# One product of 512 columns for an operand's two parts in the last feed-forward stage, and a final normalisation over transposed tokens

## The reference, cut to what matters

```python
def swiglu(h, w_in, w_out):
    gate, up = jnp.split(h @ w_in, 2, axis=-1)
    return (jax.nn.silu(gate) * up) @ w_out

def layer_norm(x):
    mu = jnp.mean(x, axis=-1, keepdims=True)
    var = jnp.mean(jnp.square(x - mu), axis=-1, keepdims=True)
    return (x - mu) * lax.rsqrt(var + EPS)

# the last two lines of the second block, last layer
x = layer_norm(ALPHA * x + 0.5 * g3 * swiglu(x * (1.0 + sc3) + sh3, ffn2_w_in[1], ffn2_w_out[1]))
return x
```

## Time and profile before

| | us |
|---|---|
| median of 3 runs | 2087.27 (2086.97 to 2087.86) |
| profiled execution | 2088.37 |
| its span (first to last instruction) | 2086.6 |
| TensorE busy | 2052.6 |
| VectorE busy | 1373.0 |
| ScalarE busy | 752.9 |
| GpSimd busy | 150.7 |

### The profile page before, as it was taken

The page is one execution under the profiler, slowest core; times in us unless marked ns, Lnnn a source line. Parts: engine busy times, 40 slices in busy tenths (PEclk is TensorE's granted clock), DMA queues, the critical chain, the costliest instruction groups (busy, mean ns, idle before and its releaser), DMA issues. The chain is left out here.

```text
span 2086.6 us, 30241 instructions
## 1 busy us (share of the span) xinstructions
PE 2052.6 (98%) x12718; PEld 1784.8 (86%) x12718; DVE 1373.0 (66%) x2160; ACT 752.9 (36%) x934; POOL 150.7 (7%) x136
## 2 busy tenths in 40 slices
PE   9999999999999999999999999999999999999998
PEld 8979979888888988688888888988888899779998
DVE  5965975776775657557776775655555565666555
ACT  4464465221222544436221222521221242555333
POOL 0400500000002000020000002000000200010001
PEclk9999999999999999999999999999999999999999
DMA  6744654554543210322554543333442333124542
GB/s 239 242 146 141 243 171 159 187 198 162 200 170 123 98 40 6 107 81 108 189 198 162 201 170 123 122 139 109 176 151 90 123 153 141 41 65 154 189 171 90
DMA packets 69280, 301.39 MB, mean 144 GB/s; under 512 B 6176, under 2 KB 24224, under 8 KB 49184
## 3 DMA queue, kind: packets, MB, share of 16 engines
q1 hardware_dynamic: 66432, 290.06, 39.2%
q10 hardware_dynamic: 2720, 9.51, 1.2%
HBM read 298.50 MB, written 1.05 MB: 144 GB/s over the span
## 5 line engine op out<-in xcount | busy, mean ns | idle before, releaser
L446 PE MATMUL PS<-xh,wh 128*128 128x512 f32 (+1 forms) x3676 | 1008.8, 349 | 2.7 <-DVE OA L1827 0.9
L446 PEld LDWEIGHTS PS<-xh,wh 128*128 128x128 f32 x3676 | 663.4, 189 | 92.6 <-issue 1.5
L446 PE MATMUL PS<-xl,wh 128*128 128x512 f32 (+1 forms) x2086 | 710.6, 341 | 0.0
L358 ACT ACTIVATE wh<-raw 128x2048 fp32r<-128x2048 f32 (+4 forms) x221 | 377.3, 1708 | 314.2 <-PE PS L446 232.3
L362 DVE TENSOR_TENSOR wh<-raw,wh 128x2048 fp32r<-128x2048 f32 (+3 forms) x183 | 376.0, 2055 | 102.2 <-ACT wh L358 101.7
L446 PEld LDWEIGHTS PS<-xl,wh 128*128 128x128 f32 x2086 | 395.2, 189 | 44.1
L446 PE MATMUL PS<-HH,wh 128*128 128x512 f32 (+1 forms) x1276 | 349.8, 360 | 0.0
L1269 DVE CUSTOM_DVE_ANT_0 NRM<-SQ,CBR 128x1024 f32<-128x1024 f32 x240 | 283.9, 1220 | 5.8
L1193 ACT ACTIVATE SI<-PS 128x512 f32<-128x512 f32 (+1 forms) x88 | 47.9, 544 | 588.2 <-PE PS L446 572.8
L446 PEld LDWEIGHTS PS<-HH,wh 128*128 128x128 f32 x1276 | 228.7, 189 | 36.5 <-DVE wh L362 0.6
L446 PE MATMUL PS<-HL,wh 128*128 128x512 f32 (+1 forms) x638 | 229.5, 360 | 0.0
(11 more groups left out here) (409 smaller groups left out, 2386.2 us busy)
## 6 DMA issues: line engine op xcount, KB each, us to landing
raw<-ffi_dram SPq DMA_DIRECT2D x88, 1024.0 KB, 4.9
SQ<-adat_dram SPq DMA_DIRECT2D x120, 512.0 KB, 4.5
raw<-ffo_dram SPq DMA_DIRECT2D x64, 704.0 KB, 4.2
raw<-layer_dram SPq DMA_DIRECT2D x36, 1024.0 KB, 4.9
lent<-layer_dram SPq DMA_DIRECT2D x14, 1024.0 KB, 7.5
raw<-odd_dram SPq DMA_DIRECT2D x12, 1024.0 KB, 4.9
raw<-even_dram SPq DMA_DIRECT2D x9, 1024.0 KB, 4.8
raw<-eout_dram SPq DMA_DIRECT2D x4, 1024.0 KB, 4.8
```

The source lines that it names most:

```text
L358: act.activation(high(i)[:, 0:n], raw[:, i.slot, 0:n], ACT.Copy).then_inc(hi_done, 1)
L446: m = pe.matmul(out, w[rows, o:o + P], x, start=n == 0 and j == 0, stop=n == len(tiles) - 1 and j == 2)
```

## The change

In stage 5 only, the input's rest is stored in the right half of the same 512-column tile as its high part (`xh`, and `HH` for the hidden values). High weights are multiplied with all 512 columns into a whole bank, the weights' rest with the left 256 columns into the left half. The right half of the bank then holds high weights times rest, and has to be added to the left half before the value is used. For input slabs ACT copies the right halves of both banks to `HF`, DVE adds them to the left halves, ACT takes Silu, DVE multiplies. For output slabs DVE adds both halves to `X` in two instructions.

At the end `X` is transposed on TensorE, 16 blocks into four banks, six chunks ahead of the column sums and two behind. The statistics lie by token on the partitions, so one instruction for each 128 tokens x 512 features does centring and scaling: two on DVE, two on ACT. Four stores of 256 KB write the result token-major; the host no longer transposes.

In `sum_late`, which stages 1 to 5 share in part, the sums of chunk 6 wait for their completion one by one (`ch.after`) instead of by the semaphore `ln_sixth`.

```diff
+        RESULT = nc.alloc_sbuf_tensor_at("RESULT", [P, 2, D], F32, offset=ends["SQ"])
...
+        def beside(pe, i, c, tiles, both, ready=None):
+            bank_ = 2 * i.par + c
+            for n, (o, k) in enumerate(tiles):
+                if ready is not None:
+                    pe.wait_ge(ready[0], ready[1] + n + 1)
+                m = pe.matmul(PS[:, bank_, :], high(i)[:, o:o + P], both[:, k, :], start=n == 0, stop=False, skip_group_check=True)
+                m = pe.matmul(PS[:, bank_, 0:T], low(i)[:, o:o + P], both[:, k, 0:T], start=False, stop=n == len(tiles) - 1, skip_group_check=True)
+            return m
+
+        def dense_beside(pe, i, chunks, kts, both, ready=None):
+            slab_begin(pe, i)
+            for c in range(chunks):
+                m = beside(pe, i, c, [((c * kts + k) * P, k) for k in range(kts)], both, None if c else ready)
+            m.then_inc(slab_used, 1)
...
-            for q in range(OUT_PARTS):
-                ks = slice(q * KT // OUT_PARTS, (q + 1) * KT // OUT_PARTS)
-                sp.wait_ge(on["x_chunk"], CHUNKS_AT[6] + ks.stop)
-                sp.dma_start(a["out"][:, ks, :], X[:, ks, 0:T]).then_inc(out_stored, 16)
+            for half in range(2):
+                for t, (sem, count) in enumerate(((on["x_chunk"], CHUNKS_AT[6]), (on["v_act"], ACTS_AT[6]))):
+                    sp.wait_ge(sem, count + half + 1)
+                    sp.dma_start(a["out"][t * P:(t + 1) * P, half * 512:(half + 1) * 512], RESULT[:, t, half * 512:(half + 1) * 512])\
+                        .then_inc(out_stored, 16)
...
+        def tokens_out(pe, chunks):
+            for k in chunks:
+                i, _ = last_slabs(5)[k]
+                pe.wait_ge(drained[i.par], i.d // 2 + 1)
+                for t in range(2):
+                    mm = pe.transpose(PS[:, TOKEN_BANKS[t][k // 4], k % 4 * P:(k % 4 + 1) * P], X[:, k, t * P:(t + 1) * P], ident)
+            if chunks.stop == KT:
+                mm.then_inc(on["row_out"], 1)
+
+        def act_result(act):
+            act.wait_ge(on["row_out"], 2 * norm_unit(5) + 1)
+            act.wait_ge(on["row_ready"], 2 * norm_unit(5) + 3)
+            for half in range(2):
+                act.activation(RESULT[:, 1, half * 512:(half + 1) * 512], PS[:, TOKEN_BANKS[1][half], :], ACT.Identity,
+                               bias=tiny[:, 132:133], scale=tiny[:, 129:130]).then_inc(on["v_act"], 1)
+
+        def dve_result(dve):
+            dve.wait_ge(on["row_ready"], 2 * norm_unit(5) + 2)
+            dve.scalar_tensor_tensor(out=tiny[:, 132:133], in0=tiny[:, 121:122], scalar=-1.0, in1=tiny[:, 129:130],
+                                     op0=ALU.mult, op1=ALU.mult).then_inc(on["row_ready"], 1)
+            dve.wait_ge(on["row_out"], 2 * norm_unit(5) + 1)
+            for half in range(2):
+                dve.tensor_scalar(RESULT[:, 0, half * 512:(half + 1) * 512], PS[:, TOKEN_BANKS[0][half], :], tiny[:, 120:121], tiny[:, 128:129],
+                                  ALU.subtract, ALU.mult).then_inc(on["x_chunk"], 1)
...
@@ pe_sums
+            if m == 5:
+                tokens_out(pe, range(0, 6))
+                column_sums(pe, u, tiles)
+                tokens_out(pe, range(6, KT))
+                return
...
@@ sum_late
-                if k == 7 and m == 4:
-                    dve.wait_ge(on["ln_sixth"], 1 + j)
                 mm = dve.tensor_tensor(NRM[:, j, 0:n], NRM[:, j, 0:n], (X, SQ)[j][:, k, 0:n], ALU.add)
-                mm.then_inc(on["ln_all" if k == 7 else "ln_sixth"], 1)
+                if k == 7:
+                    mm.then_inc(on["ln_all"], 1)
+                else:
+                    ch.after(mm)
...
@@ gate (ACT)
-                    act.activation(SI[:, i.par, 0:n], PS[:, 2 * i.par, 0:n], ACT.Silu).then_inc(on["gate_act"], 1)
+                    if m == 5:
+                        act.activation(two(HF[:, i.par, :]), PS[:, 2 * i.par:2 * i.par + 2, T:2 * T], ACT.Copy).then_inc(on["lows_in"], 1)
+                        act.wait_ge(drained[i.par], i.count(2, i.d // 2 + 1))
+                        act.activation(SI[:, i.par, 0:T], SI[:, i.par, 0:T], ACT.Silu).then_inc(on["gate_act"], 1)
...
@@ hidden (DVE)
+                    if m == 5:
+                        dve.wait_ge(on["lows_in"], half * FH + k + 1)
+                        dve.tensor_tensor(two(SI[:, i.par, :]), two(HF[:, i.par, :]), PS[:, 2 * i.par:2 * i.par + 2, 0:T], ALU.add)\
+                            .then_inc(drained[i.par], 1)
+                        dve.wait_ge(on["gate_act"], k + (h0 + 1))
+                        hf = SI[:, i.par, T:2 * T]
+                        ch.after(dve.tensor_tensor(hf, SI[:, i.par, 0:T], hf, ALU.mult))
...
@@ down (DVE)
-                    add_residual(dve, m, l, j + 2, i, k, 2 * i.par, True)
+                    if m == 5:
+                        xk, g = X[:, k, 0:T], mod[:, l, j + 2, k, 0:1]
+                        ch.after(dve.scalar_tensor_tensor(out=xk, in0=PS[:, 2 * i.par, T:2 * T], scalar=g, in1=xk, op0=ALU.mult, op1=ALU.add))
+                        dve.scalar_tensor_tensor(out=xk, in0=PS[:, 2 * i.par, 0:T], scalar=g, in1=xk, op0=ALU.mult, op1=ALU.add)\
+                            .then_inc(drained[i.par], 1)
```

More of the change, by code:

```diff
@@ L44 @@
 LENT_RING = 3
-OUT_PARTS = 4
 IN_N = 16
@@ L403, in dense_halved @@
                     wait_split(pe, i)
-                m = product(pe, PS[:, 2 * i.par + c, 0:n], i, [((c * KT + k) * P, xh[:, k, 0:n], xl[:, k, 0:n]) for k in range(KT)])
+                m = beside(pe, i, c, [((c * KT + k) * P, k) for k in range(KT)], xh)
             m.then_inc(slab_used, 1)
@@ L448, in product, with two @@
             return m
+        def two(ap):
+            return ap.rearrange("p (a t) -> p a t", a=2)
+        def beside(pe, i, c, tiles, both, ready=None):
[6 more added lines that the diff above has]
+            return m
@@ new lines, in dense_beside, with pair_beside @@
+        def dense_beside(pe, i, chunks, kts, both, ready=None):
[3 more added lines that the diff above has]
+            m.then_inc(slab_used, 1)
+        def pair_beside(pe, i, ready):
+            slab_begin(pe, i)
+            j = i + 1
+            for s, k in [(0, 0), (1, 0), (0, 1), (1, 1), (0, 2), (0, 3), (1, 2), (0, 4), (1, 3), (0, 5), (1, 4), (0, 6), (0, 7),
+                         (1, 5), (1, 6), (1, 7)]:
+                if (s, k) == (1, 0):
+                    pe.wait_ge(hi_done, HI[j.base] + 1)
+                    pe.wait_ge(drained[j.par], j.d // 2)
+                pe.wait_ge(on["xm_lo"], ready + k + 1)
+                for c in range(2):
+                    o = (c * KT + k) * P
+                    w = i + s
+                    mm = pe.matmul(PS[:, 2 * w.par + c, :], high(w)[:, o:o + P], xh[:, k, :], start=k == 0, stop=False, skip_group_check=True)
+                    if s == 0:
+                        mm = pe.matmul(PS[:, 2 * w.par + c, 0:T], low(w)[:, o:o + P], xh[:, k, 0:T], start=False, stop=k == KT - 1,
+                                       skip_group_check=True)
+                if (s, k) == (0, KT - 1):
+                    mm.then_inc(slab_used, 1)
+            wait_split(pe, j)
+            for k in range(KT):
+                for c in range(2):
+                    o = (c * KT + k) * P
+                    mm = pe.matmul(PS[:, 2 * j.par + c, 0:T], low(j)[:, o:o + P], xh[:, k, 0:T], start=False, stop=k == KT - 1, skip_group_check=True)
+            mm.then_inc(slab_used, 1)
@@ L469, in dense_pair @@
             slab_begin(pe, i)
[L470 to L487, removed]
+            for s in range(2):
+                if s:
+                    slab_begin(pe, i + s)
+                for k in range(KT):
+                    pair_terms(pe, i + s, k, n, (0, 1, 2), ready)
         def pair_in_halves(pe, m):
@@ L1225, in pe_ffn, with into @@
                 pair_in_halves(pe, m)
-            else:
-                dense_pair(pe, Idx(FIRSTS[m]), T, CHUNKS_AT[m])
+            elif m == 0:
+                dense_pair(pe, Idx(FIRSTS[0]), T, 0)
+            else:
+                pair_beside(pe, Idx(FIRSTS[m]), CHUNKS_AT[m])
+            def into(i, k):
+                if m == 5:
+                    dense_beside(pe, i, 2, KT, xh)
+                else:
+                    dense(pe, i, 2, KT, xh, xl, 0, n)
             for k in range(2, FH):
@@ L3023 @@
     a = {n: nc.dram_tensor(n + "_dram", v.shape, mybir.dt.from_np(v.dtype), kind="ExternalInput").ap() for n, v in arrays.items()}
-    a["out"] = nc.dram_tensor("out_dram", (P, KT, T), F32, kind="ExternalOutput").ap()
+    a["out"] = nc.dram_tensor("out_dram", (T, D), F32, kind="ExternalOutput").ap()
     build(nc, a)
```

67 lines of the change are left out of this document (40 added, 27 removed).

## The result

The changed kernel is slower: a ratio of 1.0032 with a 95% interval from 1.0026 to 1.0039, which is 6.7 us of 2087 (5.4 to 8.1). The medians of 18 runs each are 2093.6 and 2086.9 us. The prediction had 2092.3, 5.0 more than before. The profiled execution took 2093.87 us. The ratios of fast executions leave out one of the kernel before, of 4094 us, among its 23 beside e5 to e8.

What follows compares the result with a forecast made beforehand. TensorE, busy 98% of the span, was taken as the bound. Stage 5 +7.0, stage 4 +0.2 and the end -2.2 made +5.0 us on 2087.27: 2092.3 us, range 2088.3 to 2095.3.

Steps and rivals of the forecast that it cites:

- The chain: Stage 5 input slabs: copy, add and Silu put ACT's next high part at 1.67 us in place of 0.28.
- A: Start of ACT's first work on a slab's banks, 0.20 us after TensorE went on to the next slab.
- The waits: Stage 5: all TensorE waits added by the change, 13.6 us in sum against 6.6 gained.
- The alternation: Stage 5 input slabs: a 0.73 us wait on every second slab, lengths alternating near 5.55 and 6.28 us.
- The entry: Slabs 2 to 5 of stage 5's first half: waits of 3.75 us in sum, slab 2 starting 1.35 later.
- The second output slab of each half: Stage 5: its high part and rest come late behind the last input slab's chain, a 1.26 us wait each.
- Stage 4: Stage before the last: chunk 6's sums wait one by one, the second residual begins later, costing 0.17 us.
- The end: From DVE's last residual to the span's end: 9.1 us in place of 11.32, a gain of 2.2.
- the tile's saving: Stage 5 on TensorE: two products in place of three, 528 x 13.3 ns = 7.04 us, of which 6.61 left.
- the term of 7.0: Stage 5's last product comes 7.0 us later: 13.6 us of waits against 6.6 gained.
- Rival 3: Stage 5: fixed 13.3 ns not saved, mixed widths hiding weight loads worse; last product 10.8 us later, 2096 us; chance 0.07.
- Rival 1: Stage 5: no waits arise, as ACT and DVE have room; 8.6 us gained, 2078.7 us; chance 0.07.

Runs made afterwards that it cites:

- e5: Changed kernel plus one more ACT copy of 256 columns between the wait for DVE's add and the Silu; ratio to before 1.0059 [1.0046, 1.0072].
- e8: e4 with the narrow product ahead of the wide one in each tile; one run, 2086.2 us.
- e2: Changed kernel with the right half computed but never added, without copy, add or second residual instruction; ratio to before 0.9971 [0.9962, 0.9980].
- e4: Changed kernel, full result, with the next high part and rest (and output slabs' high part) moved ahead of other ACT/DVE work; ratio to before 0.9978 [0.9969, 0.9987].
- e1: Changed kernel with the wide product split into two of 256 columns, three products per tile; ratio to before 1.0041 [1.0027, 1.0054].
- e6: e4 with the wide product split into two of 256 columns, three products per tile; ratio to before 1.0001 [0.9992, 1.0010].
- e7: e4 with products in pairs, two wide then two narrow; ratio to before 0.9979 [0.9971, 0.9988].

## Why the prediction was right, and where it was not

**Right.** The sign and the mechanism. TensorE's saving was turned into waits for DVE's rest, the waits overtook it, and the shorter end did not make up for it.

- The chain: 1.67 predicted, 1.67 measured. The parts too: copy 0.60 where I took 0.59, add 0.69, and the high part 0.32 behind the start of a Silu of 0.42. The rest lands at A + 5.90 (5.91). e2 shows that the added instructions take 11.6 us of the stage, e4 that their place in the order does, e5 that a longer chain is paid once in two slabs.
- The waits: 13.1 us more than before by the distances between starts (13.6).
- The alternation: 12.08, 11.91 and 11.82 us for two slabs of the first half (11.83), from 1914.06 over 1926.14 and 1938.05 to 1949.87.
- The entry: high halves of slab 2 at 1892.82; after's upstream is 1.15 early, so this is 1893.97 on the time scale of before (1893.7). Slab 2 starts 1.60 later (1.35).
- The second output slab of each half: a stall of 1.14 and 1.07 beyond the usual distance (1.26 forecast). Two output slabs at the end 8.56 to 8.64 (8.60).
- Stage 4: the sums of chunk 6 and the residual behind them now start 0.46 apart, where the earlier trace rows has 0.35. From the first sum to the reciprocal it is 3.90 us in place of 3.68, +0.22 (0.17); this lies ahead of both distances of the table. The timeline of DVE:

```profile
1874.93 0.43 DVE L1220 TENSOR_TENSOR NRM<-NRM,X 128x256 f32<-128x256 f32 x1
1875.39 0.42 DVE L1220 TENSOR_TENSOR NRM<-NRM,SQ 128x256 f32<-128x256 f32 x1
1875.85 0.48 DVE L936 SCALAR_TENSOR_TENSOR X<-PS,mod,X 128x256 f32<-128x256 f32 x1
...
1878.83 0.17 DVE L1140 RECIPROCAL tiny<-tiny 128x2 f32<-128x2 f32 x1 [0.27 <-ACT tiny L625]
```

- The end: 9.11 (9.1); the reciprocal is done at 3.67 from the residual's start (3.66), the first store issued at 4.61 (4.5) and the last at 5.98 (5.7).

**Mis-sized: the tile's saving.** "The products two in place of three: 528 x 13.3 ns" is the step. The fixed part of 13.3 ns was read from streams of one width, and in a mixture it comes off whole in some stretches and by half in others. In after most tiles cost 353.3 ns, 6.7 less than 360.0; 7 stretches in 27 have the 346.7 that I forecast. So 352 tiles lose 6.7 ns each, 2.4 us, and the 496 save 4.2 us in place of 6.6. With waits of 13.1 in place of 13.6 that makes 13.1 - 4.2 = 8.9, and 8.86 is measured, 1.9 above the term of 7.0: of the 2.4 us lost on tiles 0.5 came back as shorter waits. The prediction had the two ends: with the full saving the stage would be 7.0 longer, with none 10.8, and e1 measures the second end at 10.77. Rival 3 had named this weakness, gave it nothing in between, and gave it 0.07. I had taken as evidence against it, but both of those windows have one width only and can't say anything of a mixture. Its reason, a weight load hidden worse, was not tested.

The prediction set 13.3 ns beside 2.5 ns, N/2.4 + 2.5 for a warm stream, from the Trainium skill, "TensorE: Matmul & The Clock Gate", section "Back-to-back issue gap". That section calls the formula the gap of an isolated product, and gives other figures for a stream with weight loads. No run here shows either of them.

**Rival 1** (no waits) fell: a gain is reached only with the chain taken away (e2) or put behind the next slab's parts (e4). Its reasoning from idle shares fell with it. ACT stays idle for half of each slab or more in both kernels.

**Where the expected gain went.** Out of the 6.6 us, e6 against e4 finds 4.8 to 5.5 where few waits are left. In the traces the rest is 0.4 of tiles at the higher price and 0.6 by which e4's three stalls are longer than e6's, by the distances between starts. In after's order 1.9 is left of it, and the added chain costs 10.8.

**Open.** What sets 346.7 or 353.3. Which width comes first (e8) does not decide it. Two alike in a row (e7) give a value between, 348.3, for a reason that is open too. That it changes at a slab's start and then stays suggests some alignment kept from there, which is a guess; no run set it on purpose.

## What to carry to other kernels

When a change moves work from a full engine to idle ones, find the wait that ends last for the full engine's next piece and put every added instruction into that chain: the shares of the page (36% and 66% here) say nothing about it. Then look whether the added work has to stand there. In e4 the next slab's parts came ahead of it, and 11 us hung on that order alone. Read a price from a stream of the same mixture as the one that it will be used for, and allow for values in between as well as all or nothing.

## What the runs showed of the hardware

- Products of alternating width have two prices for the same pair, 346.7 and 353.3 ns, each kept over many slabs (up to 196 tiles), where streams of one width cost 120.0 and 226.7 ns apiece. The Trainium skill, "TensorE: Matmul & The Clock Gate", section "Back-to-back issue gap", has N/2.4 + 2.5 ns as the gap of an isolated product, by which, as an estimate, a pair would take 325 ns, and about 131 ns for a product of 512 columns in a sustained stream with weight loads; no stretch here comes near either.
- The copy and the add, on the way from engine to engine, cost their own length and 0.03 to 0.04 us for each hand-over.
- A table load can run while its engine waits for a semaphore, and not ahead of the instruction in front of it: in e5 that made 1.6 us of one added instruction of 0.42.
- After TensorE had stood 2.98 us in e5, the granted clock fell to 0.50 soon after it started again, and a tile cost some 640 ns in place of 353; after 1.40 us at the same place in after it stayed at 1.00.
- The four stores of 256 KB land 2.5 us after their issue, at 354 to 415 GB/s while they run.
